# Prompt group's sparse attention: scores of 256 columns and more as three fp32r products of high and low parts, in six of eight head pairs

## The reference, cut to what matters

```python
def odd_layer_prompt(x, norm_g, w_in, w_out, ...):
    q, kc, vc, ks, vs, kw, vw, gl, z = odd_project(x, norm_g, w_in)
    kcb, vcb = compress_blocks(kc, ...), compress_blocks(vc, ...)      # 63 compressed keys
    # per block of 128 queries: all 1024/64 = 16 selected blocks fit in the top 16, so the
    # selected branch reads every key up to the query; the window branch reads the last 512
    o_cmp, o_sel = nsa_compressed_selected(q, qpos, kcb, vcb, select_blocks(ks), select_blocks(vs))
    o_win, _ = banded_attention(q, kw, vw, C_WINDOW)
    return odd_output(x, o_cmp, o_sel, o_win, gl, z, w_out)            # gates, SiLU path, projection

def masked_softmax(s, mask):                                           # s = q k^T * hd ** -0.5
    s = jnp.where(mask, s, NEG_INF)
    m = jnp.max(s, axis=-1, keepdims=True)
    p = jnp.where(mask, jnp.exp(s - m), 0.0)
    ...
```

## Time and profile before

| | us |
|---|---|
| median of 3 runs (1881.72 to 1887.7) | 1882.57 |
| the profiled execution's own time | 1888.93 |
| its span from first to last instruction | 1887.1 |
| stage of the change, from the first score to the last (PE, L1652) | 1329 to 1731 in the span |

### The profile page before, as it was taken

One profiled execution on the slowest core, in us unless ns is written; L12 is line 12 of the kernel. 1 busy time (PEld: TensorE's weight loads), 2 busy tenths in 40 slices (PEclk: granted clock), 3 DMA queues, 4 the chain that ended last, 5 costly groups with the idle time before them and its releaser, 6 DMA issues. The chain is left out here.

```text
span 1887.1 us, 35706 instructions
## 1 busy us (share of the span) xinstructions
PE 1814.0 (96%) x13758; PEld 1495.5 (79%) x13758; DVE 886.6 (47%) x2638; ACT 698.3 (37%) x1541; POOL 403.7 (21%) x575
## 2 busy tenths in 40 slices
PE   7999999999998999999999999999899999999898
PEld 6777777687875998878888787787688888888887
DVE  5322222487556444221423323333777778786534
ACT  5100000475333232000003323223677777777423
POOL 0000000000661000000005222221465555665000
PEclk9999999999897999999999999999899999999899
DMA  6434434553879663744325331444400000000564
GB/s 213 159 140 148 153 129 128 195 163 129 276 224 306 222 228 109 223 148 159 127 74 191 119 134 69 158 134 126 130 24 20 23 24 24 13 11 10 187 198 139
DMA packets 158607, 254.12 MB, mean 135 GB/s; under 512 B 33868, under 2 KB 109897, under 8 KB 154089
## 3 DMA queue, kind: packets, MB, share of 16 engines
q1 hardware_dynamic: 143976, 206.02, 34.0%
q0 software_dynamic: 4608, 33.56, 4.8%
q10 hardware_dynamic: 9856, 12.26, 2.2%
HBM read 205.88 MB, written 52.96 MB: 137 GB/s over the span
## 5 line engine op out<-in xcount | busy, mean ns | idle before, releaser
L1838 POOL TENSOR_SCALAR sparse_pr<-sparse_pr,sparse_coef,sparse_gate 128x63 f32<-128x63 f32 (+8 forms) x384 | 247.0, 666 | 177.9 <-DVE sparse_coef L1790 177.9
L1115 PE MATMUL x_acc<-x_w_hi,x_y_lo 128*128 128x478 f32 (+3 forms) x768 | 275.5, 359 | 2.3 <-DVE x_y_lo L963 2.2
L1115 PE MATMUL x_acc<-x_w_lo,x_y_hi 128*128 128x478 f32 (+3 forms) x768 | 269.8, 351 | 0.0
L1115 PE MATMUL x_acc<-x_w_hi,x_y_hi 128*128 128x478 f32 (+3 forms) x768 | 269.3, 351 | 0.0
L1729 ACT ACTIVATE sparse_pr<-sparse_pr,sparse_nmax 128x63 f32<-128x63 f32 (+8 forms) x384 | 227.1, 599 | 0.4 <-DVE sparse_nmax L1784 0.4
L489 PE MATMUL h_acc<-h_w_hi,h_y_lo 128*128 128x512 f32 x448 | 178.0, 397 | 0.8 <-DVE h_y_lo L414 0.8
L489 PE MATMUL h_acc<-h_w_hi,h_y_hi 128*128 128x512 f32 x448 | 175.3, 391 | 0.0
L489 PE MATMUL h_acc<-h_w_lo,h_y_hi 128*128 128x512 f32 x448 | 175.1, 391 | 0.0
L1115 PEld LDWEIGHTS x_acc<-x_w_hi,x_y_lo 128*128 128x128 f32 x768 | 146.4, 191 | 29.4 <-issue 14.7
L1115 PEld LDWEIGHTS x_acc<-x_w_hi,x_y_hi 128*128 128x128 f32 x768 | 146.0, 190 | 11.3
L1115 PEld LDWEIGHTS x_acc<-x_w_lo,x_y_hi 128*128 128x128 f32 x768 | 146.4, 191 | 10.4
(11 more groups left out here) (397 smaller groups left out, 3073.4 us busy)
## 6 DMA issues: line engine op xcount, KB each, us to landing
h<-cmp_w SPq DMA_DIRECT2D x56, 256.0 KB, 2.1
h_w_side<-in_even_w_in SPq DMA_DIRECT2D x16, 896.0 KB, 5.1
h_w_raw<-in_even_w_in SPq DMA_DIRECT2D x6, 2048.0 KB, 8.4
x_w_side<-in_odd_w_in SPq DMA_DIRECT2D x16, 716.0 KB, 4.7
cmp_lent<-in_odd_w_in SPq DMA_DIRECT2D x5, 1912.0 KB, 8.8
h<-x_out SPq DMA_DIRECT2D x40, 239.0 KB, 2.4
ev_unit<-in_cache_a_k SPq DMA_DIRECT2D x4, 2048.0 KB, 10.1
ev_unit<-in_cache_a_v SPq DMA_DIRECT2D x4, 2048.0 KB, 12.5
```

The lines of the kernel that those rows point to most:

```text
L1115: last = nc.tensor.matmul(acc[b][:, 0:passes[p][3]], left[:, k, t * P:(t + 1) * P], weights(right, p)[:, k, :], start=(k == 0 and a == 0), ...
L1838: nc.gpsimd.tensor_scalar(row, row, one, gate[:, t, 2 * i + e, (br + 1) % 3:(br + 1) % 3 + 1], ALU.mult, ALU.mult).then_inc(scaled, 1)
```

## The change

For the six pairs other than 0 and 4 ("split pairs" below), every score piece of more than 128 columns is computed as q_lo x k_hi + q_hi x k_lo + q_hi x k_hi in fp32r, accumulated in the same PSUM bank, for head 0 and head 1 in turn. Pieces of 128 and 63 columns, and all pieces of pairs 0 and 4, stay plain fp32.

- ACT writes `q_hi` from PSUM right behind the existing copy into `qT` (one more activation of 128x512 for each `prep` entry of a split pair), and the bank is free only after the second. DVE subtracts at the end of the same round (`cut_q`).
- The keys' high parts (ACT, two copies of 128x1024) and low parts (DVE, two subtractions of 128x1024) are made twice: for key head 0 at the end of the fifth round of pair 0 (two rounds before pair 1), for key head 1 at the end of the second round of pair 4.
- PE waits at the start of a split pair for `q_cut` and `k_cut`.
- To make room, `pr` has 58 slots and not 60, `qT` moves into memory that the next stage's rows take later (so SP waits for the last scores before it loads those), three of the eight `prT` buffers and `gate` move into the memory that holds the constants.

```diff
-    SLOTS = 60 if sparse else 44
+    SLOTS = 58 if sparse else 44
...
+    split_at = {step_of[pair_first[1]] - 2: 0, step_of[pair_first[n_pairs // 2]] + 1: 1} if sparse else {}
+    whole_pairs = (0, n_pairs // 2) if sparse else range(n_pairs)
...
+        if sparse:
+            qT = [out_loads.x[:, b, :] for b in range(2)]
+            apart = opening.spare
...
+            q_hi, q_lo = ([sb(f"{n}{b}", [P, T], F32R) for b in range(2)] for n in ("q_hi", "q_lo"))
+            k_hi, k_lo = (sb(n, [P, 2, T], F32R) for n in ("k_hi", "k_lo"))
...
+        def cut_q(dve, x):
+            dve.wait_ge(*emptied("prep", x))
+            nc.vector.tensor_tensor(q_part(q_lo, x), copied_to("prep", x), q_part(q_hi, x).bitcast(F32), ALU.subtract).then_inc(q_cut, 1)
+
+        def split_k_high(act, g):
+            if g:
+                for e in range(2):
+                    act.wait_ge(scores[e], pair_first[n_pairs // 2])
+            for m in range(2):
+                for x in range(2):
+                    act.wait_ge(*emptied("kv", (m, g, x)))
+            for m in range(2):
+                nc.scalar.copy(k_hi[:, m, :], kT_all[:, m, g, :]).then_inc(k_high, 1)
+
+        def split_k_low(dve, g):
+            for m in range(2):
+                dve.wait_ge(k_high, 2 * g + m + 1)
+                nc.vector.tensor_tensor(k_lo[:, m, :], kT_all[:, m, g, :], k_hi[:, m, :].bitcast(F32), ALU.subtract).then_inc(k_cut, 1)
...
             negated = what == "prep" and x[0] == "q"
+            if sparse and negated and x[1] not in whole_pairs:
+                nc.scalar.activation(to, src, ACT.Copy, scale=-SCALE)
+                nc.scalar.activation(q_part(q_hi, x), src, ACT.Copy, scale=-SCALE).then_inc(bank_free[entry_of[what, x] % RING], 1)
+                return
...
                     if sparse and g == len(units) // 4 - 1:
                         sp.wait_ge(stored[(g - 1) % 2], 64 * n_pairs)
+                        for e in range(2):
+                            sp.wait_ge(scores[e], n_chunks)
...
+                        if i not in whole_pairs:
+                            pe.wait_ge(q_cut, q_number(("q", i, 1)) + 1)
+                            pe.wait_ge(k_cut, 4 if i > n_pairs // 2 else 2)
...
+                        if i not in whole_pairs and b - a > P:
+                            cols = slice(blocks[0] * P + a - s0, blocks[0] * P + b - s0)
+                            for n, (q, k) in enumerate(((q_lo, k_hi), (q_hi, k_lo), (q_hi, k_hi))):
+                                for e in range(2):
+                                    half = slice(e * HD, (e + 1) * HD)
+                                    ins = nc.tensor.matmul(to[e][:, o:o + b - a], q[i % 2][half, t * P:(t + 1) * P], k[half, br, cols],
+                                                           start=n == 0, stop=n == 2)
+                                    if n == 2 and x == len(pieces) - 1:
+                                        ins.then_inc(scores[e], 1)
+                            continue
...
+                    if k in split_at:
+                        split_k_high(act, split_at[k])
...
+                    for what, x in preps[k]:
+                        if sparse and what == "prep" and x[1] not in whole_pairs:
+                            cut_q(dve, x)
+                    if k in split_at:
+                        split_k_low(dve, split_at[k])
```

More of the change, by code:

```diff
@@ L1185, in __init__ @@
         self.v_all = [x[:, 1, :, :].rearrange("p s d -> p (s d)").rearrange("p (t g d) -> p t g d", t=NT, g=2) for x in self.pieces]
-        self.con = constants(ctx, "sparse", comp.w1[1][:, :, :].rearrange("p l f -> p (l f)"))
+        wide = comp.w1[1][:, :, :].rearrange("p l f -> p (l f)")
+        self.con = constants(ctx, "sparse", wide)
+        self.q_cut, self.k_high, self.k_cut = sem("q_cut"), sem("k_high"), sem("k_cut")
+        self.spare = [wide[:, 2176 + 512 * b:2176 + 512 * (b + 1)] for b in range(3)]
+        self.gate = wide[:, 3712:4096].rearrange("p (t h x) -> p t h x", t=NT, h=16)
         self.con_in = sem("con_in")
@@ L1432, in attend_prompt @@
             q_in = [outer.pair.q_in, sb("q_in1", [P, NT, P])]
-        qT = [sb(f"qT{b}", [P, T]) for b in range(2)]
+        if sparse:
+            qT = [out_loads.x[:, b, :] for b in range(2)]
+            apart = opening.spare
+        else:
+            qT = [sb(f"qT{b}", [P, T]) for b in range(2)]
+            apart = []
         pr = sb("pr", [P, 2, SLOTS * P])
-        prT = [sb(f"prT{b}", [P, 512]) for b in range(N_T)]
+        prT = apart + [sb(f"prT{b}", [P, 512]) for b in range(len(apart), N_T)]
         warm = sb("warm", [P, 1])
@@ L1449, in attend_prompt @@
             kT_all = out_loads.lent[:, :].rearrange("p (m g c) -> p m g c", m=2, g=2)
-            gate = sb("gate", [P, NT, 16, 3])
+            gate = opening.gate
             kc_all = sb("kc_all", [P, 2, NCB])
+            q_hi, q_lo = ([sb(f"{n}{b}", [P, T], F32R) for b in range(2)] for n in ("q_hi", "q_lo"))
+            k_hi, k_lo = (sb(n, [P, 2, T], F32R) for n in ("k_hi", "k_lo"))
             vc_all = sb("vc_all", [P, 2, 2, HD])
@@ L1464, in attend_prompt @@
         scores = [sem(f"scores{e}") for e in range(2)]
+        q_cut, k_high, k_cut = (opening.q_cut, opening.k_high, opening.k_cut) if sparse else (None, None, None)
         masked, probs, coef_ready, scaled = sem("masked"), sem("probs"), sem("coef_ready"), sem("scaled")
@@ L1503, in copied_to, with q_part, q_number @@
             return o_sb[x % 2][:, :, :].rearrange("p t c -> p (t c)")
+        def q_part(split, x):
+            return split[x[1] % 2][:, x[2] * 512:(x[2] + 1) * 512]
+        def q_number(x):
+            return 2 * sum(1 for i in range(x[1]) if i not in whole_pairs) + x[2]
+        def cut_q(dve, x):
[14 more added lines that the diff above has]
+                nc.vector.tensor_tensor(k_lo[:, m, :], kT_all[:, m, g, :], k_hi[:, m, :].bitcast(F32), ALU.subtract).then_inc(k_cut, 1)
         def by_act(what, x):
@@ L2744, in attend_samples_sparse @@
         con_in = sem("con_in")
+        gathered = {(n, a): sem(f"gathered_{n}{a}") for n in ("c", "ks", "vs") for a in range(2)}
         q_all = sb("q_all", [P, NB, 64])
@@ L2789, in attend_samples_sparse @@
         gate_moved = sem("gate_moved")
-        gathered = {(n, a): sem(f"gathered_{n}{a}") for n in ("c", "ks", "vs") for a in range(2)}
         pieces_ready = [sem(f"pieces_ready{b}") for b in range(2)]
```

## The result

The changed kernel takes 1890.55 us (median of 7, 1888.26 to 1892.28) beside 1884.16 for the kernel before (7 runs, 1881.72 to 1887.7): ratio 1.0029, interval 1.0019 to 1.0040. A later timing of the same changed kernel gave 1.0015 (1.0005 to 1.0025). Both ratios are within the 0.3% that I called no change, and both intervals lie above 1: the change gains nothing and costs some 0.2%. The medians of the first timing alone lie 6.4 us apart, 0.34%, and 1890.55 is just inside the upper end of the stated range, 1891. The profiled execution took 1891.78, against 1888.93.

The account below looks back on a forecast made before the run. PE was taken to bound the stage, with ACT and DVE close behind. Terms -0.9 + 2.7 - 1.3 - 0.6 summed to -0.1 us, no change from the 1882.57 median; forecast's own range 1877 to 1891, with rival 2 1869 to 1891.

Parts of the forecast that it names:

- Bound of the kernel, products at half height: PE bounds the stage; half-height fp32r score products run side by side, saving 2.28 us a pair, 13.7 over six.
- Rival 1: Scores: fp32r halves don't run side by side; 7.5 us more a pair, 44.9 in all, 1927; chance 0.11.
- rival 3: Scores: weight loads show at half height, 5.7 us a pair against 2.3 saved; 20 slower, 1903; chance 0.07.
- Point A: Round 2: ACT's added activation frees the `prep` bank later; margin 0.05 us, PE waits 0.85.
- Point B: Round 4: ACT's first copy comes late for PE's second score bank; margin 0.12 us, loss 0.62.
- Pairs 3 and 7: Split pairs preparing a whole pair or none: waits of 0.37, 0.14 and 0.43 us; gain 1.34 each.
- Rival 2: ACT and DVE give way, so all 13.7 us less 0.6 arrives: 1869.5; chance 0.14.
- Point C: Round 5: `cut_q` stands between DVE's reciprocal and the accumulator's copy before PE's `out`; PE waits 1.03 us.
- Pair 0 and the keys' split: Pair 0: one `cut_q` shows behind DVE's masks, 0.6 us lost; keys' split costs nothing, up to 8.4 if uncovered.
- Moves: 58 slots, moved buffers and SP's new wait: no cost.

Follow-up runs that it names:

- e5: Changed kernel, with ACT making the queries' high part later from the finished copy and DVE's second-half subtraction two rounds later: 1878.27 us against 1885.26, ratio 0.9960.
- e3: Changed kernel with the three fp32r products all reading high parts and no low parts made: 1879.94 us, ratio 0.9964 to the kernel before.
- e2: Changed kernel making all high and low parts, but with every score a plain fp32 product: 1894.0 us, ratio 1.0041 to the kernel before.
- e4: Changed kernel with DVE's query subtraction ahead of the round's reciprocals, not behind them: 1882.66 us, ratio 0.9986 to the kernel before.
- e7: Changed kernel run again without an edit, beside the kernel before: 1887.31 us against 1885.26, ratio 1.0015.
- e8: e5 plus, in two-unit rounds, the second unit's reciprocal moved behind the next round's turn copies: 1873.12 us against 1885.26, ratio 0.9935.
- e1: Changed kernel with only the memory moves and SP's new wait, no pair split: 1884.4 us against 1886.11 for the kernel before, ratio 0.9993.
- e9: Kernel before with e8's deferred reciprocals alone, no fp32r scores: 1883.56 us against 1884.26, ratio 0.9996.
- e6: Changed kernel with DVE's query subtraction as four of 128 columns, not one of 512: 1895.77 us in one run.

## Why the prediction came out as it did

The forecast was no change, put at 1882.7 on a median of 1882.57. By the ratios it came out 0.29% and 0.15% slower, 5.5 and 2.8 us. Of this the stage holds 2.9 between the two profiled executions (446.69 - 443.82), where the sum had 0.1. That a missed term of this size still left "no change" true is luck of a kind: 0.3% of this kernel is 5.6 us, wide enough for it.

- **Bound of the kernel, products at half height: right.** 227 ns at full height became 0.23 at half height for both heads together, loads hidden. Rounds 1, 3 and 6, which PE sets, are shorter by 0.40, 0.28, 0.33 (predicted 0.42, 0.26, 0.31). Rivals 1 and 3 fell: the two heads' products of 512 columns start 8 ns apart (median in the trace), and no load is visible. The rule of the Trainium skill, "TensorE: Matmul & The Clock Gate", Part 3, that I weighed for rival 3 would have put loads in view; the trace disagrees at half height too: loads of 0.18 us run under products that follow each other in 0.23.
- **Point A: right.** Place to the transpose; round 2 +0.47 against +0.53 for pair 1. e5, which frees the bank earlier, brings it to +0.09.
- **Point B: right.** +0.16 against +0.07 in pair 1; +0.35 against +0.36 in pair 4.
- **Pairs 3 and 7: right.** -1.27 and -1.32 against -1.34. e3 shows the same in all six split pairs. Rival 2, that ACT and DVE give way, fell with that: rounds 2 and 5 gave back their savings, and round 4 a third of its own, with no added work at all.
- **Point C: right in place and mechanism; the term of the sum was mis-sized.** The prediction said: "The new `cut_q` stands between reciprocal and copy. PE waits 0.55 (round 4's saving) + 0.60 - 0.12 = 1.03." For the 0.60 it took a subtraction from the earlier trace rows, a place in which POOL was not at work. Here the reciprocal in front of `cut_q` waits for ACT's exponentials just after POOL has been released by the reciprocal before it, so POOL's scaling runs when `cut_q` starts. The four that started inside an instruction of POOL took 1.37, 1.38, 1.49 and 1.37 us: 4 x 0.69 less, that is 2.85 too much, and the stage is 2.8 longer than forecast. That these two agree so well is in part chance: the four pairs are 2.7 above the forecast, pair 0 is 0.33 below it, and start and end add 0.4. Pairs 1, 2 and 5 are 0.69, 0.69 and 0.63 above, and pair 4 0.7; pair 6, whose `cut_q` began first, is not. Its sum agrees, but not its rounds: round 4 is 0.29 above (0.27 of it a pause between score products for which the trace names no cause) and round 5 0.29 below.
- **Pair 0 and the keys' split: the place was right, the sum is not separated.** I priced pair 0 at 0.6 and the split at nothing. The 0.6 is there: PE's wait for DVE's masks in round 3, 3.78 in the earlier trace rows, is 4.38 (at 1347.23) and also 4.38 in e2, e4, e5, e7 and e8, and stays 3.78 in e1, e3 and e9, which have no `cut_q`. The whole start is only 0.36 longer, so part of it is absorbed or lies in the scatter. Its last two rounds are 0.27 longer. The low part of key head 0 took 1.91 for 1.22, as it too met POOL. e2 has +1.24 in these rounds and e5 +0.27. e2 is one of the three traces with the shorter start, and the other two also lose more in round 5 of pair 0 (+0.43 and +0.32); that the one makes the other is likely and not shown.
- **Moves: right.** e1.
- **Open:** the first ratio is 0.29% where the profiled stage accounts for 0.15%. The repeat gave 0.15%. I saw no other place that had changed, and take it as scatter; that is not shown.

**Where the expected gain went.** The product pieces save 13.7 us of PE time (12.5 measured on the page). About 1.0 of each pair's 2.28 is lost without any added work (e3), to ACT and DVE, which already finished just in time for rounds 2, 4 and 5. The added work at A, B and C takes the rest, and half of what is taken at C is POOL's. Placed elsewhere (e5) it costs nothing, and with DVE's wait moved out of the way (e8) the change is worth 0.65% of the time, 12.3 us of stage and 10.6 of it in the rounds, the fastest of all kernels run. What still doesn't arrive is round 2.

## What to carry to other kernels

When a saving on the bounding engine adds instructions to others, look up where these instructions land in the order of each engine, not how busy the engine is: the same 0.69 us cost 1.3 behind one instruction and nothing ahead of it. Price an operation by a row taken under the same neighbours: a DVE operation that reads two SBUF operands costs up to one POOL instruction more (two in e8) wherever POOL is at work. And where an engine waits just before the critical copy, that wait is the place for the added work, or the thing to move.

## What the runs showed of the hardware

- **DVE against POOL.** A DVE subtraction of 128x512 with both inputs in SBUF: 0.68 to 0.69 us with POOL idle, 0.65 to 0.68 where POOL's instruction is the one that waits; 1.37 to 1.49 when it starts inside one of POOL's scalings of 896 columns and waits, ending 0.54 after that ends; 2.13 to 2.20 when it lets two pass (e8). Of 128x128: 0.28 and 0.96 to 1.09. Of 128x1024: 1.22 and 1.91. In the other direction POOL's 896-column scaling is lengthened from 1.09 to 1.52 and 1.54, one of 63 columns from 0.41 to 0.92. DVE's copy out of PSUM ran beside POOL at its usual length (`oT`, 0.68 at 1409.74, POOL busy).
- **fp32r at half height.** Two products of 64 rows side by side: 0.23, 0.18 and 0.12 us for 512, 384 and 256 columns, within 4 ns the same N/2.4 + 14 ns as one at full height.
- **The clock.** After one wait of PE of 2.46 us (e6, pair 2) the granted clock was 0.50 for 3.4 us; after waits of 2.48 us at the same place of pairs 5 and 6 it stayed at 1.00, as after all of 1.5 to 2.1 us there. Near the end of the stage one wait of 2.46 us stands in all eleven traces: in nine the clock falls to 0.50 for 3.4 us, between 0.3 before and 1.8 us after the wait's end; in e2 and e7 it stays at 1.00, and these two ends are 1.0 to 1.7 us shorter. So the length of the wait alone doesn't decide it; what does, no run here shows. Between two profiles of one kernel this alone made 1.7 us.
